# Rebuilding the bidirectional state-space mixing of a two-layer encoder on one core: one product per log-decay tile, chunk pairs joined directly, y feature-major, loops written out

## The reference, cut to what matters

```python
# y_t = sum_{s<=t} C_t.B_s exp(sum_{s<u<=t} dt_u A) dt_s x_s
seg = a_cum[:, :, :, None] - a_cum[:, :, None, :]
decay = jnp.exp(jnp.where(tril, seg, -jnp.inf))
scores = jnp.einsum("bcign,bcjgn->bcijg", Cc, Bc)
y_diag = jnp.einsum("bcijgr,bcjgrp->bcigrp", scores[..., None] * decay, xdt)
states = jnp.einsum("bcjgn,bcjgrp->bcgrpn", Bc, xdt * decay_to_end[..., None])
...
y_off = jnp.einsum("bcign,bcgrpn->bcigrp", Cc, prev) * jnp.exp(a_cum)[..., None]
...
y_fwd = _ssd_scan(xs, dt[:, :, 0], A[0], Bm, Cm)
y_bwd = flip(_ssd_scan(flip(xs), flip(dt[:, :, 1]), A[1], flip(Bm), flip(Cm)))
y = y_fwd + y_bwd + xs * D_skip.astype(xs.dtype)[:, None]
y = _gated_group_rms_norm(y.reshape(bsz, l, SSD_INNER), p_z, norm_g)
```

## Time and profile before

| | |
|---|---|
| time, median of 3 runs (range) | 3090.6 us (3089.87 to 3091.07) |
| the profiled execution: time, span | 3091.98 us, 3090.5 us |
| TensorE | 3014.7 us (98%), 13,916 products |
| its weight loads | 2499.7 us (81%) |
| VectorE | 1909.0 us (62%) |
| ScalarE | 1210.4 us (39%) |
| GpSimd | 88.8 us (3%) |
| transfers | 298.34 MB, 97 GB/s on average |
| mean granted TensorE clock | 0.99 of 2.4 GHz |

### The profile page before, as it was taken

How to read it: one execution, slowest core, us unless ns; L and a number is a source line. 1 busy time by engine, 2 the same in 40 slices (tenths; PEclk the granted TensorE clock), 3 DMA queues, 4 the chain that set the end, 5 groups by cost and what they waited for, 6 DMA issues and landing times.

```text
span 3090.5 us, 41274 instructions
## 1 busy us (share of the span) xinstructions
PE 3014.7 (98%) x13916; PEld 2499.7 (81%) x13916; DVE 1909.0 (62%) x2503; ACT 1210.4 (39%) x1611; POOL 88.8 (3%) x186
## 2 busy tenths in 40 slices
PE   7999989999999999999999998999999999999998
PEld 5888868888887787888878887888888877878886
DVE  5444578999993555444544445799899735554444
ACT  4322344445543434222342224444554444252223
POOL 0000000000000000000000000000000010000000
PEclk9999999999999999999999999999999999999999
DMA  4333322323234433333333332332333353333332
GB/s 144 95 95 95 96 69 83 97 85 89 84 95 124 132 103 89 102 95 96 96 96 95 95 95 82 85 86 82 95 91 89 86 167 98 96 88 98 99 92 78
DMA packets 523803, 298.34 MB, mean 97 GB/s; under 512 B 10399, under 2 KB 514215, under 8 KB 523687
## 3 DMA queue, kind: packets, MB, share of 16 engines
q1 hardware_dynamic: 511888, 261.65, 29.6%
q0 software_dynamic: 10176, 34.63, 3.3%
q10 hardware_dynamic: 1623, 0.55, 0.1%
HBM read 277.92 MB, written 18.87 MB: 96 GB/s over the span
## 4 chain that ended last, share of the span: by engine, by line
PE 94%; DVE 2%; issue 1%; ACT 1%; DMA 1%; DVEq 0%; ACTq 0%; SPq 0%; POOLq 0%; POOL 0%
PE bank L1139 84%; PE bank L1264 2%; PE bank L1254 2%; PE bank L1249 1%; PE bank L1251 1%; PE bank L1337 1%; PE bank L1330 1%; DMA yraw<-y_spill 1%; PE bank L1307 0%; PE bank L1361 0%; PE bank L1297 0%; PE bank L1274 0%; PE bank L1313 0%; DVE bc L949 0%; DVE acc L776 0%
## 5 line engine op out<-in xcount | busy, mean ns | idle before, releaser
L1139 PE MATMUL bank<-uhi,whi 128*128 128x512 f32 x2944 | 1166.3, 396 | 29.6 <-DVE ulo L807 21.6
L1139 PE MATMUL bank<-uhi,wlo 128*128 128x512 f32 x2944 | 1150.6, 391 | 0.0
L1139 PE MATMUL bank<-ulo,whi 128*128 128x512 f32 x2944 | 1149.3, 390 | 0.0
L765 DVE TENSOR_TENSOR wlo<-wraw,whi 128x1024 fp32r<-128x1024 f32 x496 | 605.5, 1222 | 307.7 <-ACT whi L445 297.1
L445 ACT ACTIVATE whi<-wraw 128x1024 fp32r<-128x1024 f32 x496 | 521.1, 1053 | 433.2 <-PE bank L1139 433.0
L1139 PEld LDWEIGHTS bank<-uhi,whi 128*128 128x128 f32 x2944 | 555.4, 189 | 150.0 <-issue 28.4
L1139 PEld LDWEIGHTS bank<-uhi,wlo 128*128 128x128 f32 x2944 | 554.8, 188 | 118.0
L1139 PEld LDWEIGHTS bank<-ulo,whi 128*128 128x128 f32 x2944 | 555.6, 189 | 113.3 <-issue 1.4
L1139 PE MATMUL bank<-hhi,whi 128*128 128x512 f32 x960 | 377.1, 393 | 7.4 <-DVE hlo L1041 4.1
L1139 PE MATMUL bank<-hhi,wlo 128*128 128x512 f32 x960 | 374.2, 390 | 0.0
L1139 PE MATMUL bank<-hlo,whi 128*128 128x512 f32 x960 | 374.2, 390 | 0.0
(11 more groups left out here) (199 smaller groups left out, 2144.8 us busy)
## 6 DMA issues: line engine op xcount, KB each, us to landing
wraw<-in_ffn_w_up SPq DMA_DIRECT2D x179, 512.0 KB, 3.7
wraw<-in_w_in SPq DMA_DIRECT2D x160, 512.0 KB, 3.8
wraw<-in_ffn_w_down SPq DMA_DIRECT2D x64, 512.0 KB, 3.7
wraw<-in_ssd_w_out SPq DMA_DIRECT2D x32, 512.0 KB, 3.8
wraw<-in_ffn_w_down SPq DMA_DIRECT2D x32, 384.0 KB, 3.3
y_spill<-yz POOLq DMA_DIRECT2D x16, 512.0 KB, 3.1
yraw<-y_spill POOLq DMA_DIRECT2D x32, 256.0 KB, 3.5
wraw<-in_conf_w_out SPq DMA_DIRECT2D x16, 512.0 KB, 4.3
```

Source lines behind the costliest of these rows:

```text
L765: v_.tensor_tensor(wlo[:, t % RING, :], wraw[:, t % RING, :], f32(whi[:, t % RING, :]), ALU.subtract).then_inc(lo_ready, 1)
L1139: ins = t_.matmul(out, a[:, slot, w], b[:, at + k, :], start=start and k == 0 and a is whi and b is hi, stop=stop and k == nk - 1 and a is ...
```

## The change

The SSD of a group is done per request r (two) instead of per chunk:

- The prefix sums are set up once per layer in `Q` (sums, with rows of ones), `Lr` and `LX` (the same, less log dt; with rows of ones). For each group ScalarE multiplies `Q` by a column of a selector (`selm`) for each head and direction, 16 copies of 256 columns (`selected`), into `R`. One product `Lr`.T x `R` then gives a log-decay tile for four heads (`seg_diag`), with the mask as a second product.
- The pair of chunks across is one more product of the same kind, with `LX` (`seg_cross`), so there are no states, no `xw`, no `yoff`. Scores are now made for the whole request per chunk (256 columns).
- y is the product of `xT` (64 columns as weights) and `M` (256 tokens moving), accumulated over both chunks, straight into feature-major partitions 0 to 63 or 64 to 127 (`y_rows`): no transposes.
- ScalarE takes six exponentials per request instead of four; two of them are taken in place in PSUM, and VectorE adds them from there (`both_ways`), then multiplies by the scores 1,024 wide (`scored`).
- VectorE writes the 31-tap input directly into one of two padded buffers `vp`; the result is written back there and stored from there.
- The loops over layers and groups are written out on all engines, SP's loops too; the slab loops inside the FFN stay on PE, DVE and ACT.

The core of the diff (in the order POOL, ScalarE, VectorE, TensorE after the first lines):

```diff
-    ND, NA = 16, 6
...
+    ND, NA = 19, 4
...
+    EPR, EPG = 6, 12
...
-        TAP_SLICES = [(0, 8), (8, 14), (14, 18), (18, 23), (23, 27), (27, 29), (29, DWK), (DWK, DWK)]
+        TAP_SLICES = [(0, 8), (8, 14), (14, 18), (18, 23), (23, 25), (25, 25), (25, 29), (29, DWK)]
...
-                with sp.Fori(0, NG) as g:
+                for g in range(0, NG):
...
-                    pool.dma_start(vp[:, :, HALO:HALO + SEQ],
-                                   v_dram[:, bass.ds(g - 1, 1)].rearrange("r o p t -> p (r o) t")).then_inc(vp_in, 16)
...
-                    pool.dma_start(v_dram[:, bass.ds(g, 1)].rearrange("r o p t -> p (r o) t"),
-                                   tg[:, :].rearrange("p (r t) -> p r t", r=2)).then_inc(v_out, 16)
...
+                    pool.wait_ge(unit_done, U + 1)
...
+                    pool.dma_start(c_dram[:, g - 1:g].rearrange("r o p t -> p (r o) t"),
+                                   vp[:, U % 2, :, HALO:HALO + SEQ]).then_inc(c_out, 16)
...
+                def selected(r):
...
+                    need(act, seg_ps, H * EPG + r * EPR)
+                    for d in range(2):
+                        for h in range(HPG):
+                            head = (g - 1) * HPG + h
+                            a_.activation(R[:, d, :, h, :], f32(Q[:, d, 2 * r:2 * r + 2, :]), ACT.Copy,
+                                          scale=selm[:, head:head + 1]).then_inc(rs_ready, 1)
...
+                def decay(r, e):
+
+                    act.wait_ge(seg_ps, H * EPG + r * EPR + e + 1)
...
+                    a_.activation(dst, src[:, :].rearrange("p (h i) -> p h i", h=HPG), ACT.Exp).then_inc(e_ready, 1)
...
+                    if ssd and t == 0:
+                        selected(0)
...
+                    if ssd and t in (1, 3):
+                        for e in range(4):
+                            decay(t // 2, e)
+                    if ssd and t in (2, 4):
+                        for e in range(4, EPR):
+                            decay(t // 2 - 1, e)
+                    if ssd and t == 2:
+                        selected(1)
...
+                def both_ways(r):
+
+                    for c in range(2):
+                        dve.wait_ge(e_ready, H * EPG + r * EPR + 2 * c + 2)
+                        part = M[:, r, c, :, c, :]
+                        v_.tensor_tensor(part, part, bank[3 + 4 * c][:, :].rearrange("p (h i) -> p h i", h=HPG), ALU.add).then_inc(m_added, 1)
+
+                def scored(r):
...
+                        part = M[:, r, c, :, :, :].rearrange("p h c i -> p h (c i)")
+                        v_.tensor_tensor(part, part, SC[:, 2 * r + c, :].unsqueeze(1).broadcast_to([P, HPG, SEQ]), ALU.mult).then_inc(m_ready, 1)
...
+                        dve.wait_ge(c_out, max(G - 1, 0) * 16 + 16)
+                        v_.scalar_tensor_tensor(out=vp[:, G % 2, :, HALO:HALO + SEQ], in0=tg[:, :].rearrange("p (r t) -> p r t", r=2), scalar=1.0,
+                                                in1=bank[1][:, :].rearrange("p (r t) -> p r t", r=2), op0=ALU.add, op1=ALU.mult).then_inc(v_ready, 1)
...
+                v_.memset(vp[:, :, :, :], 0.0).then_inc(pad_zero, 1)
+                v_.memset(f32(Q[2 * NH:P, :, :, :]), 1.0).then_inc(ones_set, 1)
+                v_.memset(f32(Lr[0:2 * NH, :, :, :]), 1.0).then_inc(ones_set, 1)
+                v_.memset(f32(LX[0:2 * NH, :, :]), 1.0).then_inc(ones_set, 1)
...
+                def seg_diag(r):
...
+                    for c in range(2):
+                        for d in range(2):
+                            out = heads(2 + 4 * c + d)
+                            t_.matmul(out, Lr[:, d, 2 * r + c, :], R[:, d, c, :, :], start=True, stop=False)
+                            t_.matmul(out, identr[:, :], never[:, d, :].unsqueeze(1).broadcast_to([P, HPG, P]),
+                                      start=False, stop=True).then_inc(seg_ps, 1)
+
+                def seg_cross(r):
+
+                    for c in range(2):
+                        pe.wait_ge(e_ready, H * EPG + r * EPR + 2 * c + 1)
+                        t_.matmul(heads(2 + 4 * c), LX[:, 2 * r + c, :], R[:, c, 1 - c, :, :], start=True, stop=True).then_inc(seg_ps, 1)
+
+                def y_rows(r):
...
+                    for j in range(2):
+                        for c in range(2):
+                            for half in range(2):
+                                h = 2 * j + half
+                                ins = t_.matmul(bank[4 + r][half * HEAD:(half + 1) * HEAD, j * SEQ:(j + 1) * SEQ],
+                                                xT[:, 2 * r + c, h * HEAD:(h + 1) * HEAD],
+                                                M[:, r, c, h, :, :].rearrange("p c i -> p (c i)"), start=c == 0, stop=c == 1)
```

More of the change, by code:

```diff
@@ L276, in ffn @@
                 for p0, n in PARTS:
-                    with sp.Fori(0, n // 2) as i:
+                    for i in range(0, n // 2):
                         for q in range(4):
@@ L281, in ffn @@
                     s = s + 2 * n
-                    with sp.Fori(0, KD // 4) as i:
+                    for i in range(0, KD // 4):
                         for q in range(4):
@@ L293, in columns @@
                              w[:, bass.ds(L * KD, 8), bass.ds(i * (4 * P) + (q * P + col), P)])
-            with sp.Fori(0, DEPTH) as L:
+            for L in range(DEPTH):
                 ffn(L, 0, 0)
-                with sp.Fori(0, NG) as g:
+                for g in range(0, NG):
                     s = L * NSLAB + g * 8 + S_GROUP
@@ L304, in _ @@
                 columns(L, S_GA, W_IN, C_GA)
-                with sp.Fori(0, KD // 2) as i:
+                for i in range(0, KD // 2):
                     for q in range(4):
@@ L675, in y_hi @@
                 a_.activation(dst, yraw[:, k % 4, :], ACT.Copy).then_inc(yhi_ready, 1)
-            with act.Fori(0, DEPTH) as L:
+            for L in range(DEPTH):
                 ffn(L, 0, 0)
@@ L688, in _ @@
                     a_.activation(uhi[:, k, :], sq[:, k % 2, :], ACT.Copy).then_inc(nhi_ready, 1)
-                group(L, 0, True, False, False)
-                group(L, 1, True, True, False)
-                with act.Fori(2, NG) as g:
-                    group(L, g, True, True, True)
+                for g in range(NG):
+                    group(L, g, True, g > 0, g > 1)
                 def gate_b(t):
@@ L1041, in y_lo @@
                 v_.tensor_tensor(lo[:, k % KD, :], yraw[:, k % 4, :], f32(hi[:, k % KD, :]), ALU.subtract).then_inc(y_split, 1)
-            with dve.Fori(0, DEPTH) as L:
+            for L in range(DEPTH):
                 ffn(L, 0, 0)
@@ L1258, in y_chunks, with heads @@
[L1258 to L1275 removed]
+                def heads(b):
+                    return bank[b][:, :].rearrange("p (h i) -> p h i", h=HPG)
@@ L1366, in _ @@
                 ins.then_inc(slab_done, 1)
-                group(L, 0, True, False, False)
-                group(L, 1, True, True, False)
-                with pe.Fori(2, NG) as g:
-                    group(L, g, True, True, True)
+                for g in range(NG):
+                    group(L, g, True, g > 0, g > 1)
                 group(L, NG, False, True, True, gate=0)
```

456 lines of the change are left out of this document (167 added, 289 removed).

## The result

The changed kernel takes 2995.09 us (median of four runs, 2994.31 to 2999.35) where the kernel before took 3090.84 on the same chip: a ratio of 0.9691, 95% interval 0.9674 to 0.9708. The forecast was 3022.6 with a range from 3004 to 3056.

A forecast was written before the change was run, and what follows sets the result against it. TensorE bounds the kernel before; VectorE would bound the changed middle groups. Middle groups 46.8, g=1 10.8, g=8 8.4, edges 2.0 make 68.0 us; 3092.0 less that and 1.4 gives 3022.6, range 3004 to 3056.

The forecast's parts named there:

- What bounds before: Middle groups of the kernel before: TensorE sets the 61.89 us, and VectorE follows, waiting 3.3 us per group for it.
- TensorE's sum: TensorE's products per middle group: 16.0 us go out, 10.6 come in by the lower price, leaving 56.5 us.
- The y visit: TensorE's 16 passes of 64-column y products: 1.94 us if the array's halves overlap; two visits per group.
- the open price: Cost of the 32 y passes per group on TensorE: 6.91 us one after the other, 3.89 if halves overlap.
- the lower end: y passes on TensorE: array halves work side by side because products alternate output partitions; 3.89 us per group, the price taken.
- VectorE's own round: VectorE in a middle group: 58.6 us of own work with small bubbles, 1.4 less after the change, so 57.2.
- The new wait: VectorE's decay additions wait about 0.8 us for exponentials, in a chain starting at its sum of squares; group becomes 58.0.
- Rival 2: ScalarE's scaled copies cost 0.61 us each and come late, TensorE waiting for R: 3045 us; chance 0.08.
- g=8: Each layer's group without a new convolution: 5.4 us won less 1.2 of TensorE waiting on table loads, 8.4 for two.
- The edge and group 0: Layer's edge wins 4.0 us (2.7 pause, 1.3 clock); VectorE's new fills cost group 0 1.0 us per layer, 2.0.
- 1: Rival: the array's halves do not overlap in the y products, TensorE stays the bound at 59.5 us: 3053 us; chance 0.30.
- 3: Rival: written-out code is not there in time, each pause 2.71 us; two per group give 3130 us; chance 0.04.
- 4: Rival: VectorE's strided additions and wide multiplications cost half as much again, 3.5 us more per group: 3071 us; chance 0.03.

The follow-up runs named there:

- the fastest version: Changed kernel with convolutions' first taps on ScalarE at step ends, first request's copies in step 4 (group 1's unmoved), three fills in step 1: 2988.66 us.

## Why the prediction was right, and where it was wrong

**What bounds before: right.** The kernel before written out gives VectorE 1.4 us per group and the group keeps its 61.89.

**TensorE's sum: close.** Forecast 56.5, measured 55.83. What comes in is as priced: scores 1.77 (8.09 - 5.44 less the x transposes at 0.88), diagonal 2 x 1.84, across 2 x 0.45, y 2 x 2.10, together 10.55 against 10.6. The y visit was the open price, and the lower end was the right choice: 1.88 us for 16 passes, and the run with the halves in turn shows that the alternation, the reason given for it, is what makes them cheap. The Trainium skill (TensorEngine Tiling (Array Packing), Key Properties) says that different tiles can execute weight loads and matmuls in parallel. The trace agrees, as long as neighbours in the queue write different halves: 1.88 us, against 2.79 with four and four.

So it is the removed work that was put too low: 10.55 + 6.06 = 16.6 went, not 16.0. The missing 0.6 are the changeovers from the removed visits back to the slab, which I counted only for the new ones. The trace of before shows them. After each of the seven visits in a group the slab's second product starts 0.28 to 0.42 us after its first, not 0.227, as here after the y products:

```profile
870.38 0.48 PE L1139 MATMUL bank<-uhi,whi 128*128 128x512 f32 x1
870.69 0.39 PE L1139 MATMUL bank<-ulo,whi 128*128 128x512 f32 x1
```

Together that is 0.66 us per group, of which only the 0.09 behind the scores and transposes stays.

**VectorE's own round: this is the step that failed.** "Of its 61.89 us, 3.3 are waits for TensorE, so its own work, with its small bubbles, is 58.6" carried the small bubbles over into the changed kernel. The change of work was right: 1.4 us less forecast, 56.80 - 55.32 = 1.48 measured. But the bubbles were register instructions of the loop, and the diff writes the loop out. They went with it: 1.25 us per group by the loop put back, 1.4 by the kernel before written out. With the loop put back the twelve middle groups take 12.3 us more, so that is some 12 of the 22 us missed there. Another 4 are g=2, counted like the others: in it VectorE is still ahead and TensorE's 55.8 holds, twice, instead of 58.0. I priced the written-out loops at the layer's edge only; 99 register instructions per group stood in the trace before, between the operations that I did read.

**The new wait: right in place, too long, and its source was wrong.** 0.27 us and not 0.8, with 0.20 in step 5 unforeseen: 0.33 less in a group, another 3 to 4 us over the groups that have it. What is left of the 22, some 2 us, is not traced. I let the chain begin at VectorE's sum of squares. It begins at the silu of x, earlier in ScalarE's queue, and the scaled copies lie on it. "With 29.82 of 61.89 us busy there is room" was wrong as an argument: a doubled set of copies costs 3.2 of its 3.3 us. Rival 2 had the right engine and the wrong victim; it looked at TensorE waiting for R, which it does not do.

**g=8: wrong by 1.5 us each.** The 1.2 us of TensorE waiting for table loads did not come; g=8 has the middle groups' length, since it starts as late as VectorE left group 7 (in the fastest version, where VectorE is not late, it takes 55.83). TensorE's 0.6 from the changeovers is in it too.

**The edge and group 0: right in sum, the edge with some luck.** 4.2 for 4.0, but the pause alone gave 3.2 where 2.7 stood, and the clock about 0.9 where 1.3 stood, a part that changes by 1.6 us from one execution to another (last section). Group 0 has its 1.0 per layer, though three fills explain only half of it.

**The rivals.** 1 is out (1.88 us per visit), 3 is out (no such pause in the groups; by the loop put back, rolled code costs more here), 4 is out: the wide multiplications take 1.14 us each and an addition from PSUM 0.60, as priced. The range failed at its lower end because that end took TensorE at 56.5 for the floor of all groups (and with g=8's 1.2 still taken off: 16 x 5.4 by itself gives 3002, not 3004). With the measured 55.83 the same sum, 16 x 6.06 and 2.0 more, gives 2992, below the measured 2995. So two terms were mis-sized in the same direction: VectorE's bubbles in the forecast, and TensorE's changeovers in the range.

## What to carry to other kernels

When a diff writes a loop out, count the register instructions between an engine's operations in the trace of before: they cost nothing while the engine still waits for another, and become a term of the sum as soon as that engine is the next bound. And once several engines are near the limit, busy time per window no longer names the bound: follow the round, from a wait of one engine through the other's queue back to the same instruction one group later, and add it up; an engine that is idle a third of the time can own a stretch of it. A single lightened load that changes the time less than it should, as the four taps did, is how such a round shows.

## What was not expected of the hardware

Register instructions on VectorE showed as gaps of 0.145 us between dependent taps and cost 1.25 to 1.4 us in a group of about 56 us of work. The Trainium skill (Perfetto Trace Analysis, Sequencer Loop) says that the sequencer starts a control instruction itself, where it only queues an instruction of the engine. By that the gaps are plausible; their size is from the runs.

Products with 64 weight columns overlap by the order in which they are queued: alternating halves 1.88 us for 16 passes, four and four 2.79.

At the layer's edge TensorE's pause fell from 5.67 to 2.43 us. An equal pause opens the second FFN. After such a pause some eight products can come 0.427 us apart instead of 0.227 (the 1.2 GHz level; the granted clock of that slab's window is 0.82 and not 1.00), which costs 1.6 us. In most profiled executions of written-out kernels this follows exactly one of the two pauses, and that is why the table adds the two stretches: the changed kernel opened layer 2 in 7.81 us and had the loss in the FFN, the fastest version the other way round, 9.42 us. But the run with four taps less had it after both (373.5 us for the two stretches together), and that with the copies twice after neither (370.3). So 1.6 us between two runs here can be chance. What decides it no run shows.
